# The z columns of a hybrid decoder layer: per head in eight token blocks, or for all heads ahead of them by Strassen's seven products

## The reference

```
u    = rmsnorm(h, norm_w)                       # (1040, 1024)
proj = u @ w_in ;  z = proj[:, 4096:5120]       # 1024 x 1024 x 1024 for the real tokens
y    = ssd_scan(...) + xs * d                   # (1040, 1024), in 4 groups of 256
y    = groupnorm(y * silu(z)) * ssm_norm_w
```

## Time and profile before

| | |
|---|---|
| timed runs, median | 1036.84 us |
| profiled execution, span from the first to the last instruction | 1035.9 us |
| PE busy | 1010.1 us |
| DVE busy | 622.6 us |
| ACT busy | 443.3 us |
| POOL busy | 253.3 us |
| granted TensorE clock, mean | 0.993 |

### The profile page before, as it was taken

One profiled execution on the slowest core, in us unless ns is written; L12 is line 12 of the kernel. 1 busy time (PEld: TensorE's weight loads), 2 busy tenths in 40 slices (PEclk: granted clock), 3 DMA queues, 4 the chain that ended last, 5 costly groups with the idle time before them and its releaser, 6 DMA issues.

```text
span 1035.9 us, 16326 instructions
## 1 busy us (share of the span) xinstructions
PE 1010.1 (98%) x6177; PEld 923.2 (89%) x6177; DVE 622.6 (60%) x1199; ACT 443.3 (43%) x1020; POOL 253.3 (24%) x222
## 2 busy tenths in 40 slices
PE   3999999999999999999999999999999999999997
PEld 3889989998999999989999999899999898888885
DVE  7555766446257664462576644625766536798866
ACT  6333444343434343434343344343433544543555
POOL 3012331233223412332224133322241330000002
PEclk8999999999999999999999999999999999999999
DMA  8012322221143232211422322114223203994313
GB/s 271 1 45 82 102 80 78 69 62 52 45 129 102 66 88 72 62 43 40 144 91 69 92 76 62 42 41 143 74 75 98 77 24 106 364 385 143 101 52 163
DMA packets 105945, 101.22 MB, mean 98 GB/s; under 512 B 6022, under 2 KB 79852, under 8 KB 105868
## 3 DMA queue, kind: packets, MB, share of 16 engines
q1 hardware_dynamic: 105868, 100.18, 30.2%
HBM read 79.11 MB, written 21.05 MB: 97 GB/s over the span
## 4 chain that ended last, share of the span: by engine, by line
PE 95%; DVE 2%; ACT 1%; issue 1%; DMA 1%; POOL 0%; DVEq 0%; SPq 0%; ACTq 0%
PE ps L1614 51%; PE ps L1623 15%; PE ps L1815 9%; PE ps L1599 5%; PE ps L1780 3%; PE ps L1829 2%; PE ps L1758 2%; PE ps L1759 2%; PE ps L1831 1%; PE ps L1835 1%; PE ps L1706 1%; PE ps L1781 1%; PE ps L1800 1%; DMA conv_u<-in_norm_w 1%; PE ps L1762 0%
## 5 line engine op out<-in xcount | busy, mean ns | idle before, releaser
L1614 PE MATMUL ps<-u_hi,w_hi 128*128 128x348 f32 (+3 forms) x1024 | 364.3, 356 | 1.8 <-POOL w_lo L908 1.8
L1614 PE MATMUL ps<-u_lo,w_hi 128*128 128x348 f32 (+3 forms) x1024 | 348.1, 340 | 0.0
L1614 PE MATMUL ps<-u_hi,w_lo 128*128 128x348 f32 (+3 forms) x1024 | 347.4, 339 | 0.0
L908 POOL TENSOR_TENSOR w_lo<-w_raw,w_hi 128x1024 fp32r<-128x1024 f32 (+1 forms) x56 | 122.8, 2193 | 343.7 <-ACT w_hi L998 271.7
L1614 PEld LDWEIGHTS ps<-u_hi,w_hi 128*128 128x128 f32 x1024 | 193.9, 189 | 13.5 <-POOL w_lo L908 2.1
L1614 PEld LDWEIGHTS ps<-u_hi,w_lo 128*128 128x128 f32 x1024 | 193.2, 189 | 11.0
L1614 PEld LDWEIGHTS ps<-u_lo,w_hi 128*128 128x128 f32 x1024 | 193.6, 189 | 10.3
L899 POOL TENSOR_TENSOR small<-small,m_half 128x1 f32<-128x1 f32 (+2 forms) x57 | 41.3, 727 | 332.0 <-DVE small L1553 143.0
L1388 DVE TENSOR_REDUCE small<-ps 128x1 f32<-128x144 f32 (+7 forms) x64 | 49.6, 774 | 90.4 <-PE ps L1762 89.9
L1815 PE MATMUL ps<-w_hi,u_hi 128*128 128x256 f32 x256 | 73.1, 286 | 0.0
L1815 PE MATMUL ps<-w_lo,u_hi 128*128 128x256 f32 x256 | 72.0, 281 | 0.0
(11 more groups left out here) (302 smaller groups left out, 1741.1 us busy)
## 6 DMA issues: line engine op xcount, KB each, us to landing
w_raw<-in_w_in SPq DMA_DIRECT2D x56, 512.0 KB, 4.1
acum_b<-acum_scratch SPq DMA_DIRECT2D x32, 256.0 KB, 4.3
acum_b<-in_w_out SPq DMA_DIRECT2D x22, 256.0 KB, 4.2
work<-in_w_out SPq DMA_DIRECT2D x16, 256.0 KB, 4.0
t_scratch<-work SPq DMA_DIRECT2D x16, 256.0 KB, 2.2
t_scratch<-acum_b SPq DMA_DIRECT2D x16, 256.0 KB, 2.6
y_scratch<-ys SPq DMA_DIRECT2D x8, 512.0 KB, 4.0
work<-in_x SPq DMA_DIRECT2D x4, 1024.0 KB, 8.5
```

Of the source, the lines that this page charges most:

```text
L908: eng.tensor_tensor(w_lo[:, a % 2, ks, :], w_raw[:, a % 2, ks, :], w_hi[:, a % 2, ks, :].bitcast(F32), ALU.subtract).then_inc(w_lo_ok, 1)
L1614: ins = eng.matmul(dst, w[:, k, 0:m], u[:, k, cols], start=(k == 0 and n == 0), stop=(k == KD - 1 and n == 2))
```

## The change

z is no longer made in the heads. The 1024 x 1024 product for the 1024 real tokens is split into 2 x 2 blocks of 512 and made by seven products of 512 x 512 x 512 (Strassen in Winograd's form, as in the output projection), for all heads at once, ahead of the first head. Each product is four slices (`ZK`) by four token blocks by three terms, 48 matmuls of 512 columns; seven are 336, where 768 of 256 columns stood.

- Weight blocks T1 to T4 (1 MB each) are loaded in the token stage (`z_weights`), and POOL forms the sums of weights in place (`z_sum`, 128x1024 each).
- The sums of tokens: s1 by ACT (a copy out of PSUM) and DVE (L1473) in the token stage, s2 by POOL (blocks 0, 1) and DVE (2, 3), s3 and s4 by POOL, two operations for each of eight slices.
- Products 1 and 2 (`M_11`, `M_12`) are steps `z_early`, three matmuls each; one stands between a tile's two half transposes, two behind them, from tile 2 on. What is left of them follows the stage. The token transposes, casts and subtractions are cut in halves, and PSUM banks 2 and 3 take the two halves of every tile.
- The other five products are PE's `z_run()`, with their own lists for ACT (`Z_ACT`) and DVE (`Z_DVE`), and lists for POOL and SP. Four outputs of 512 x 512 are gathered (`z_acc`, `z_add`), gated (`z_tanh`, `z_gate`) and stored in DRAM (`z_store`). A head loads its 256 columns with one DMA of 1 MB (`z_load`) at the end of its attention.
- K's and Q's first pieces move from between the transposes to behind z (`PRE`).
- In the heads the convolution's first four half pieces take the place of the first four z steps; behind them only `PAUSE` = 1 empty unit and the rest of the pieces are dealt out.
- Constants that stood at the program's start (three memsets) move behind z, since buffers are shared; `norm_row` and `x_buf` have other places.

```diff
-    add("z", 1)
+    emit(conv[0])
     spare(1)
     add("o_scale", 1)
-    add("z", 2)
+    emit(conv[1])
     spare(2)
-    add("z", 3)
+    emit(conv[2])
     add("attn_out", 1)
     ...
-    add("z", 4)
+    emit(conv[3])
     add("chunk", 0)
     add("decay", 1)
-    units = [[("z", a, 0)] for a in range(5, QB + 1)]
-    units[-1].append(("split", TCB, 0))
-    units += [[]] * PAUSE
+    units = [[]] * PAUSE + conv[4:]
...
-PAUSE = 4
+PAUSE = 1
...
+def ahead():
...
+    early = list(Z_EARLY)
+    for r in range(-3, CH):
...
+        if r >= 5:
+            out.append(("s1", r - 5))
+        if r + 1 in range(CH):
+            out.append(("x_turn", (r + 1, 0)))
+            out += [("z_early", early.pop(0)) for _ in range(1 if r > 0 else 0)]
+            out.append(("x_turn", (r + 1, 1)))
+            out += [("z_early", early.pop(0)) for _ in range(Z_PER_TURN - 1 if r > 0 else 0)]
...
+            def z_run():                                        # POOL
+                iteration(-1, [("s2", 0, 1), ("s2", 1, 1), ("z_sum", ("T2", 1), 1), ("z_sum", ("T3", 0), 1), ("z_sum", ("T3", 1), 1),
+                               *[("s3", (M_S3, k), 1) for k in range(ZK)], ("z_sum", ("T4", 0), 1), ("z_sum", ("T4", 1), 1),
+                               *[("s3", (M_S4, k), 1) for k in range(ZK)]])
...
+                        if q == 0:
+                            eng.wait_ge(z_out_ok, 4)
+                            eng.wait_ge(s2d_ok, 2)
+                        if q >= 2:
+                            eng.wait_ge(s_lo_ok[M_S3 if q - 2 < ZK else M_S4], (q - 2) % ZK + 1)
+                        own(eng, eng.tensor_tensor(s_f[q % 2], u_hi[:, ZK + k, cols].bitcast(F32), s2_f[:, k, :], ALU.subtract))
+                        eng.tensor_tensor(s_f[q % 2], s_f[q % 2], u_lo[:, ZK + k, cols].bitcast(F32), ALU.add).then_inc(s3_ok, 1)
...
+            def z_run():                                        # PE
+                for n in range(Z_TURNED, Z_SLOTS):
+                    p, j = divmod(n, ZK)
+                    eng.wait_ge(z_lo_ok, n - Z_TURNED + 1)
...
+                    for t in range(4):
+                        if p == M_S2 and j == 0:
+                            eng.wait_ge(s_lo_ok[p], t + 1)
+                            eng.wait_ge(z_acc_ok, z_kept(0, t))
+                        if p == M_S1 and j == 0:
+                            eng.wait_ge(z_acc_ok, z_kept(3, t))
...
+                        ins = z_multiply(n, t)
```

More of the change, by code:

```diff
@@ L64, in pieces_of @@
     return [(PW * n, min(PW * (n + 1), L)) for n in range(PIECES)]
-COLS = {t: pieces_of(t) for t in range(NT) if t not in (TZ0, TZ1)}
+COLS = {t: pieces_of(t) for t in range(NT)}
 FIRST_OF, WHOSE = {}, {}
 for _t in range(NT + 1):
-    FIRST_OF[_t] = len(WHOSE) + (QB if _t > TZ1 else 0)
+    FIRST_OF[_t] = len(WHOSE)
     for _n in range(len(COLS.get(_t, ()))):
         WHOSE[FIRST_OF[_t] + _n] = (_t, _n)
-PZ = FIRST_OF[TZ0]
 PPI = FIRST_OF[NT]
-assert PZ % 2 == 0 and PPI % 2 == 0
+assert PPI % 2 == 0
 NQ, NK, NG, NGC = (len(COLS[t]) for t in (TQ, TK, TG, TGC))
@@ L155, with z_done, z_kept @@
 assert len(FIRST) == first_piece(TXS0)
[L158 to L167, removed]
+ZK = KD // 2
+Z_SLOTS = 7 * ZK
+ZX_BANKS, ZY_BANKS = (0, 1, 4, 7), (5, 6, 2, 3)
+Z_BANKS = (ZX_BANKS, ZY_BANKS, ZX_BANKS, ZX_BANKS, ZY_BANKS, ZX_BANKS, ZY_BANKS)
+Z_BLOCKS = {"T3": (0, 0), "T4": (1, 0), "T1": (0, 1), "T2": (1, 1)}
+Z_OF = ("T3", "T4", "T2", "T1", "T3", "T2", "T4")
+Z_TURNED = 8
+Z_OUT = ((0, 0), (1, 1), (0, 1), (1, 0))
+Z_READ = (M_12, M_S2, M_S3, M_S4, M_22)
+Z_EARLY = [(p, t, j) for p in (M_11, M_12) for t in range(4) for j in range(ZK)]
+Z_PER_TURN = 3
+def z_done(n):
+    p, j = divmod(n, ZK)
+    if p == M_11:
+        return "z_k", 1
+    if p in Z_READ and (j == ZK - 1 or p == M_12):
+        return "z_bank", 4 * (Z_READ.index(p) + 1)
+    return "z_k", 1 + sum(1 for m in range(2 * ZK, n + 1) if not (m % ZK == ZK - 1 and m // ZK in Z_READ))
+def z_kept(o, t):
+    return 4 * (0, 3, 1).index(o) + t + 1
 def piece(t, tc):
@@ L298, in schedule @@
                 break
-        units += conv
         jobs.pop()
-    else:
-        units += conv + half_pieces([TQ, TK, TV], 1)[0]
+    add("o_mean", 1)
+    emit(conv[0])
+    spare(1)
+    add("o_scale", 1)
+    emit(conv[1])
+    spare(2)
+    emit(conv[2])
+    add("attn_out", 1)
+    add("store_attn")
+    spare(9)
+    add("decay_load", 1)
+    add("decay_load", 2)
+    emit(conv[3])
+    add("chunk", 0)
+    add("decay", 1)
+    units = [[]] * PAUSE + conv[4:]
+    jobs = [(n + PAUSE - 4, job) for n, job in jobs]
+    if not last:
+        units += half_pieces([TQ, TK, TV], 1)[0]
     slots = LAST_FILL if last else SCAN_FILL
@@ L667, in build @@
         out_k = sem("out_k")
[L668 to L669 removed]
+        x_res = [[x_in[2 * n + m] for m in range(2)] for n in range(2)]
+        fin_in = x_in[4]
         out_bank = sem("out_bank")
```

459 lines of the change are left out of this document (337 added, 122 removed).

## The result

The changed kernel takes 1049.52 us (median of 4 runs, 1047.82 to 1050.82), the kernel before in the same session 1036.86 (1036.62 to 1037.24). The ratio is 1.012, 95% interval 1.0105 to 1.0134: slower by 1.2%. The forecast was 1045.4 in a range of 1023 to 1055 with slower as the likeliest sign; the sign came, and the time is inside the range, 4.1 us above the likeliest value. The profiled execution spans 1046.7 us, 10.8 more than the one before; it is one of the two shorter of the four runs, whose spans are 1046.1 to 1049.1.

The account below looks back on a forecast made before the run. PE (TensorE), busy for 98% of the span, was taken to bound the kernel. 94.8 - 91.7 + 5.5 = +8.6 on the 1035.9 us span gave 1044.5; with 0.9 for the median, 1045.4 us, range 1023 to 1055.

Parts of the forecast that it names:

- t0: End of the token stage's last low half, plus 1 us for TensorE's clock: 42 us, bounds 39 and 48.
- z's stalls: PE's waits in z ahead of products 3 to 6: 7.4 + 5.6 + 5.0 + 1.0 = 19.0 us.
- K's and Q's first pieces: Matmuls moved from the token stage to behind z, all exposed now: 9.4 us.
- dt begins: Point where the dt matmuls start, used to compare kernels: 133.8 us against 39.0, so +94.8.
- z removed: z's matmuls taken out of the four heads, 22.9 us each on the chain: 91.7 us less.
- so 0.2 us on each of eight steps: Last head: a norm needs 2.0 us and a hand-over against a half piece of 1.9, so 0.2 us stall per step.
- The heads' sum: Stalls in the heads once z's cover is gone, 4 x 1 + 1.5: +5.5 us, bounds 0 and 12.
- 2 (hardly any exclusion): In z, POOL and DVE hardly delay one another: 1025.7 us, range 1020 to 1034.8; chance 0.25.
- 3 (half): In between, a draw with half of those stalls in z: 1034.8 to 1038.9 us; chance 0.12.
- The sign that was to decide for 2: Stalls in z below 10 us would decide for POOL and DVE hardly delaying one another.
- 4 (the clock): TensorE's clock stays at the lower level through the token stage: 1052.5 us, all of it 1059; chance 0.10.
- the forecast's own case: t0 from 40 to 45, stalls in z 14 to 23, heads 3 to 8: 1038.9 to 1055 us; chance 0.53.

Follow-up runs that it names:

- the last version: Changed kernel with s3, T3 and T4 sums on DVE, orders mended, projection loads later in the last head, fifth convolution half piece behind chunk 1: 1032.32 us.
- its best version: Changed kernel with s3, T3 and T4 sums on DVE, orders mended, last head's loads later, fifth convolution half piece behind chunk 1: 1032.32 us, ratio 0.995 to kernel before.

## Why the prediction came out right, and where its steps were off

- **The sign, and its reason.** z ahead of the heads costs more on PE than it saves in them, because seven products of PE time come with waits for operands that DVE and POOL must make in turns. Eight unused POOL operations put where POOL was idle cost 6.5 us. Moving POOL's s3 to DVE took DVE's lows behind it back to 0.69 in both runs that did it; by itself, with s3 alone, it gained no time (2.7 more), and 7.7 us only with ACT's order changed too. So the turns are shown as a cause, and order is the other one.
- **t0: 42 predicted, 44.1 measured.** The 1 us allowed for the clock was about right: with a full clock the same code has 43.0, so the low clock took 1.1. The last scale ended at 37.8, where 37.2 was reckoned, although beside POOL's z lows scales took 2.09 and 1.85 instead of 1.28, and the last one, behind T1's second half, 3.28. What was mis-sized is the tail behind it: 3.6 us reckoned, 6.3 measured, 5.1 of them at full clock. The last transposes also waited for DVE's s1 operation (0.68, released at 39.6), and between their two halves stands a group of three z matmuls (0.70); neither was in the 3.6.
- **z's stalls: 19.0 predicted, 9.2 measured.** PE's own work was 66.6 for 63.4 reckoned, 2.2 of it low clock; products 6 and 7 took 22.25 for 96 matmuls, 0.232 each. "TensorE: Matmul & The Clock Gate" of the Trainium skill, section "Back-to-back issue gap", states about 131 ns for such a matmul; the changed kernel's trace does not agree with it either, at a granted clock of 1.00. For the first stall, 7.4 was expected and 3.89 came (5.24 where PE arrived at full clock): POOL reached T2's second half at 45.18, 1.1 behind t0, where the working had it at s2(1) until t0 + 4.2. It had run through s2 while DVE was busy from PSUM or waiting for ACT. A pair of 0.6 + 1.28 was reckoned with 1.88 and took about 1.7. With the earlier start, z_low 12 was there 26.7 us behind t0 and z_low 20 53.5, where the working had 30.7 and 60.1, and the other stalls were 3.09, 1.91 and 0.34 against 5.6, 5.0 and 1.0.
- **K's and Q's first pieces: 9.4 predicted, 3.81 + 5.57 = 9.4 measured.** Sum at "dt begins": +94.8 predicted, +90.3 measured.
- **z removed: -91.7, and 1 us a head for scan 0.** Exact in the body: 22.92 - 21.93 = 0.99 us, of which the chain's landmark has 0.7 as PE's wait for xdd.
- **The last head is the term that was mis-sized**, "so 0.2 us on each of eight steps", with 1 for scan 0: 2.5 predicted, 9.1 measured. The step reasoned from a norm of 2.0 us against a half piece of 1.9, as if every norm were like the one in the earlier trace rows. Three were not, since other work stood ahead of a link of their chains: out_load on SP (3.60), the last weights on POOL (1.33), the convolution on DVE (1.44). 6.5 us of waits more than before and some 1.7 of low clock (0.83 over 860 to 870) make 8.2 of the 9.1; the rest I did not find. The loads' share is shown by an experiment; the shares of POOL's weights and of the convolution are read from the timelines. The heads' sum, 5.5 with bounds 0 and 12, measured 12.1. The prediction said of z_load on SP that it costs nothing, which is so, but did not ask what else in that queue would lose its slack: delaying the output projection's loads gave 5.0 of the 9.1 back.
- **Rivals.** 2 (hardly any exclusion) and 3 (half) fall by the lengths, 1.78 and 2.87 where 0.69 was the mark. The sign that was to decide for 2, stalls in z below 10 us, came all the same, with 9.2: it was a bad sign, since the walk overstated the stalls with the mechanism right. 4 (the clock) falls, with 1.00 over 14 to 40. A smaller cost of that kind came behind waits: 1.1 us of t0, nearly all of which z's first wait would have taken anyway, 1.7 in z and 1.7 in the last head.
- **Luck in the sum.** The two errors, -4.5 ahead of the heads and +6.6 in them, partly cancel, so the sum (+8.6 for +10.8) was better than its terms. Of the three terms in the forecast's own case, only t0 lies in the stretch given for it (40 to 45); z's stalls of 9.2 lie below 14 to 23, and the heads' 12.1 above 3 to 8. The low end of that case was also added up wrongly: t0 of 40, stalls of 14 and heads of 3 make 1035.9, not 1038.9. Of the distance from 1045.4 to the median another 1.9 us is the changed kernel's own spread: its profiled execution is 2.8 below its median, where before it was 0.9.

Left open: what remains of z's time in the last version, with 111.2 - 50.9 - 55.8 = 4.5 us more than PE's own 5 x 11.16 between product 3's start and the K piece, of which PE's waits explain 2.6; and whether other splits of the sums between POOL and DVE in the token stage would shorten t0, which was not tried.

## What to carry to other kernels

Moving arithmetic off the bounding engine pays only if the operands' preparation fits under it. Add up POOL and DVE work with SBUF operands as one queue, not as two half idle engines, and lay POOL's work beside DVE's work from PSUM. When a block of matmuls is taken out, look in the profile for every chain that it covered: here the order of a load queue, which had cost nothing, became 3.6 us of wait, and one half piece in the wrong place 10 us. Between the changed kernel and its best version lie 17 us, all from which engine makes a sum and in which order steps and loads stand: more than the difference between the two kernels, and what turned 1.2% slower into 0.5% faster.
